# Splitting the router off the second norm in a transformer block: raw logit rows, a shift row through DRAM, and a gather by token tiles

## The chip, the cores and the metric

The kernel runs on one core of a Trainium2 chip. The metric is the device time in microseconds (us), the median of three runs. The engines are PE (TensorE), DVE (VectorE), ACT (ScalarE), POOL (GpSimd) and SP (SyncE, here only a queue of DMA issues).

## The reference, cut to what matters

One layer on 256 tokens of width 1024: an adaptive norm, a sparse attention branch and a gated linear attention branch, then a mixture of 32 experts, 4 for each token. Float32 throughout. The change lies at the seam between the branches and the experts:

```python
mod = (silu(c) @ w_ada + b_ada)                      # sh1, sc1, gt1, sh2, sc2, gt2, 1024 wide each
x = x + gt1 * (merged @ w_out)
h2 = _rmsnorm(x, norm2_g) * (1.0 + sc2) + sh2
x = x + gt2 * _moe(h2, ...)

def _moe(h, ...):
    logits = xt @ router_w + router_b
    top_v, top_e = lax.top_k(logits, TOP_K)          # TOP_K = 4 of 32
    wts = softmax(top_v)
    ... tokens sorted by expert; for each block of one expert:
        hgu = xb @ w_gate_up[e] + b_gate_up[e]       # 1024 -> 2048
        act = (min(gate, 7) * sigmoid(1.702 * gate)) * (clip(up) + 1)
        y = act @ w_down[e] + b_down[e]              # 1024 -> 1024
```

The expert weights are 12 MB for each expert, 384 MB in all, and every expert is read.

## The kernel before

The kernel is written engine by engine with semaphores set by hand. 256 tokens are two tiles of 128 (t = 0, 1), the width is two halves of 512. A list PLAN gives the order in which PE fills the eight PSUM banks by name (`wo0`, `hh0`, `rl1`, ...) and says whether ACT or DVE takes each out.

**Front part.** SP loads the weights in pieces of 2 MB into four buffers; each piece waits until PE (or DVE, for the `ada` pieces) has used the one before it in its buffer (L397). DVE multiplies the eight `ada` pieces of the six modulation rows by silu(c) (`weigh`, L1066), PE adds the partitions up with a matrix of ones (`add_parts`, L1549; tiles `ab0` to `ab7`) and DVE adds the bias (`take_sum`, L1021): `ab0`, `ab1` give gt1, `ab2`, `ab3` the shift sh2, `ab4`, `ab5` the scale sc2g, `ab6`, `ab7` the gate gt2.

**The seam.** PE makes `wo0` and `wo2` (token tile 0), then `wo1` and `wo3` (tile 1), L1574. `take_wo` (L1047) on DVE forms the residual x2 and x2 times sc2g. ACT takes the sum of squares (`square_sum`), `second_norm` (L1056) makes the inverse root and the finished rows h2. PE transposes h2 (`hh0` to `hh3`), multiplies with the router's weights in four row groups (`rp`), ACT copies the partial sums (`rpart`) and PE adds them up (`rl`, L1598). DVE picks the top four (`chosen`), PE counts (`rt`), DVE finds the slot of each token with expert 0 (`sel`, L1164), and PE gathers the rows of expert 0's block (`gather`, L1613). PE matmuls called `keep_busy` fill its waits. `router_weights` (L1147) makes the softmax weights; POOL splits them into three bf16 parts (L553 to L558) and only then begins to copy experts. h2 is also split in three bf16 parts, by `round_part` on ACT and `subtract_part` (L1114) on DVE.

**The experts.** Expert 0 comes in 12 loads of 1 MB straight into its slots. Each later expert comes in six units of 2 MB into three landing buffers in turn (`land`, L391), and POOL copies each unit in two halves into the slots (L566) as PE is done with them. The unit after next can only be issued when POOL has emptied its landing buffer. The first three units wait for other things: unit 0 for all of h2 and the gate, unit 1 for `rl1`, unit 2 for `gather` and for `left` of both tiles (L1120). Units 3, 4 and 5 wait for POOL's copies of units 0, 1 and 2. A loop over blocks of 64 rows then runs `gate_up` (L1688) and `down` (L1738).

Of the kernel before, what the change touches and what calls it, by code (L numbers as in the profile page):

```python
# [15 lines left out]
P = 128  # L16
# [54 lines left out]
def hybrid_block(nc, x, c, w_ada, b_ada, norm1_g, w_in, w_gate_lr, b_gate, gla_norm_g, w_branch_a, w_branch_b, w_out,  # L71
# [27 lines left out]

    with ExitStack() as ctx:  # L100
# [13 lines left out]
        bd = sb("bd", 96, [P, D])  # L114
# [45 lines left out]
        gt2 = sb("gt2", 180, [P, D])  # L160
# [56 lines left out]
        wts4 = sb("wts4", 187.5, [P, TT, 2, E])  # L217
# [6 lines left out]
        rpart = sb("rpart", 152, [P, T])  # L224
        first_used = small("first_used", [1, 1], I32)
# [55 lines left out]
        landing = [sb(f"landing{i}", at, [P, 2, 2048]) for i, at in enumerate((168, 152, 104))]  # L281
        fgl = sb("fgl", 168, [P, D])
# [34 lines left out]
        first_count_ready = sem("first_count_ready")  # L317
        gu_used = [sem(f"gu_used{j}") for j in range(8)]
# [56 lines left out]
        def _(sp):  # L375
# [94 lines left out]
        def _(pool):  # L470
# [31 lines left out]
            for part, dst in ((2, gt1), (3, sh2), (5, gt2), (4, fgb)):  # L502
                pool.dma_start(dst[:], b_ada[0:1, part * D:(part + 1) * D].to_broadcast([P, D])).then_inc(brow_in, 16)
# [4 lines left out]
            for i in range(4):  # L508
                pool.dma_start(bd[E * i:E * (i + 1), :], b_down[0]).then_inc(bd_in, 16)
# [33 lines left out]
            pool.wait_ge(bias3_ready, 1)  # L543
            for q in range(2):
                step.settle()
                step(nc.gpsimd.tensor_copy(gt2q[64 * q:64 * q + 64, :], gt2[64 * q:64 * q + 64, 512 * q:512 * q + 512]), gate_ready)
            pool.wait_ge(bd_in, 64)
            step.settle()
            step(nc.gpsimd.tensor_tensor(bd[:], bd[:], gt2[:], ALU.mult), gate_ready)

            pool.wait_ge(wts_ready, TT)
# [24 lines left out]
        def _(act):  # L576
# [256 lines left out]
        def _(dve):  # L833
# [184 lines left out]
            dve.wait_ge(brow_in, 64)  # L1018
            chain(V.scalar_tensor_tensor(fgb[:], fgb[:], 1.0, sc2g[:], ALU.add, ALU.mult))

            def take_sum(r):  # L1021

                cols_ = slice(512 * (r % 2), 512 * (r % 2) + 512)
                dst = (gt1, sh2, sc2g, gt2)[r // 2][:, cols_]
                wait_tile(dve, f"ab{r}")
                if r // 2 == 2:
                    chain(V.tensor_tensor(dst, tile(f"ab{r}")[:], dst, ALU.mult))
                    step(V.tensor_tensor(dst, dst, fgb[:, cols_], ALU.add), out_dve)
                else:
                    step(V.tensor_tensor(dst, tile(f"ab{r}")[:], dst, ALU.add), out_dve)  # L1030


# [14 lines left out]
            def take_wo(i):  # L1047
                cc, t = divmod(i, TT)
                xv = xs[:, t, 512 * cc:512 * cc + 512]
                wait_tile(dve, f"wo{i}")  # L1050
                chain(V.tensor_tensor(tmp[:], tile(f"wo{i}")[:], gt1[:, 512 * cc:512 * cc + 512], ALU.mult), out_dve)
                chain(V.tensor_tensor(x2[t][cc][:], xv, tmp[:], ALU.add), x2_ready)
                cols_ = slice(512 * cc, 512 * cc + 512)
                step(V.tensor_tensor(h2[:, t, cols_], x2[t][cc][:], sc2g[:, cols_], ALU.mult))

            def second_norm(t):  # L1056
# [3 lines left out]
                inverse_root(1, D, (x2ss_ready, 2 * t + 2), x2var_ready, x2root_ready, first=t)  # L1060
                for half in range(2):
                    cols_ = slice(512 * half, 512 * half + 512)
                    step(V.scalar_tensor_tensor(h2[:, t, cols_], h2[:, t, cols_], rs[:, t:t + 1], sh2[:, cols_],
                                                ALU.mult, ALU.add), h2_ready)
# [59 lines left out]
            subtract_part(1, 0)  # L1124
            take_wo(3)
            second_norm(1)
# [3 lines left out]
            for i in range(3):  # L1130
                step(V.memset(ypart[i][:], 0.0), ypart_ready[i])
            step(V.memset(zrow[:], 0.0), zrow_ready)
            dve.wait_ge(numbers_ready, 1)
            step(V.tensor_scalar(esel[:], ones[0:3 * E, 0:SLOTS], expert_no[:], None, ALU.is_gt), esel_ready)

            step(V.memset(lg[:, :, E:E + TOP_K], PAD))
# [10 lines left out]
            def router_weights(t):  # L1147
# [7 lines left out]
                step(V.tensor_copy(wts4[:, t, :, :], wts[:, t, :].unsqueeze(1).to_broadcast([P, 2, E])), wts_ready)  # L1155

            router_weights(0)
            wait_tile(dve, "rt")
            for t in range(TT):
                step(V.scalar_tensor_tensor(first_slot[:, t:t + 1], tile("rt")[:, t * E:t * E + 1], 1.0, chosen[:, t, 0, 0:1],  # L1160
                                            ALU.add, ALU.mult))
            step.settle()
            for t in range(TT):
                ins = V.tensor_scalar(sel[:, t, :], slot_no[:], first_slot[:, t:t + 1], None, ALU.is_equal)  # L1164
            ins.then_inc(sel_ready, 1)
# [21 lines left out]
            router_weights(1)  # L1187
# [3 lines left out]
            subtract_part(0, 1)  # L1191
# [7 lines left out]

            subtract_part(1, 1)  # L1200
# [23 lines left out]
            dve.wait_ge(gate_ready, 3)  # L1224
# [57 lines left out]
        def _(pe):  # L1282
# [61 lines left out]
            def transposes(name, src, t, half):  # L1344
                ps = begin(name)
                for j in range(4):
                    a = (4 * half + j) * P
                    ins = nc.tensor.transpose(ps[:, j * P:(j + 1) * P], src[:, t, a:a + P], ident[:])
# [199 lines left out]

            def add_parts(r):  # L1549
# [13 lines left out]
            for kind, src in (("gm", hT), ("wa", yaT), ("wb", ybT)):  # L1563
                for cc in range(2):
                    by_feature(kind, cc, src)
                    add_parts(r - 1)
                    r += 1
            pe.wait_ge(merged_ready, 4)
            for t in range(TT):
# [6 lines left out]
                if t == 0:  # L1576
                    add_parts(7)

            pe.wait_ge(late_in, 48)
            pe.wait_ge(bias3_ready, 1)  # L1580
            for t in range(TT):
                if t:
                    keep_busy(tile("rp0"), 4)
                for half in range(2):
                    pe.wait_ge(h2_ready, 2 * t + half + 1)
                    transposes(f"hh{2 * t + half}", h2, t, half)
                ps = begin(f"rp{t}")
                keep_busy(ps, 3 if t else 7)
# [7 lines left out]
                M(ps[:, 0:E], ones[0:1, :], rb[:], start=True, stop=False)  # L1596
                wait_out(pe, f"rp{t}")
                full(M(ps[:, 0:E], rpart[:, t * P:(t + 1) * P], stack[:], start=False, stop=True))  # L1598

            ps = begin("rt")  # L1600
            keep_busy(ps, 5)
            pe.wait_ge(chosen_ready, 1)
            M(ps[:, 0:E], before[:], chosen[:, 0, 0, :], start=True, stop=True)
            M(ps[:, E:3 * E], ones[:], chosen[:, 0, 0:2, :], start=True, stop=False)
            pe.wait_ge(chosen_ready, 2)
# [7 lines left out]
            def gather(into):  # L1613

                for t in range(TT):
                    for q in range(2):
                        ins = M(into[64 * q:64 * q + 64, :], sel[:, t, :], h2[:, t, 512 * q:512 * q + 512],
                                start=(t == 0), stop=(t == TT - 1))
                ins.then_inc(gath_full, 1)
# [31 lines left out]
            def weight_transposes():  # L1651

                pe.wait_ge(wts_ready, TT)
                nc.tensor.transpose(x_bank[:, 0:P], wts4[:].rearrange("p t q e -> p (t q e)"), ident[:]).then_inc(wt_full, 1)
# [16 lines left out]
            def bias_rows():  # L1671

                for i in range(4):
                    t, q = divmod(i, 2)
                    M(sum_bank[t][q][:], wT[E * i:E * (i + 1), :], bd[E * i:E * (i + 1), 512 * q:512 * q + 512], start=False, stop=False,
# [78 lines left out]
            pe.wait_ge(gate_ready, 3)  # L1754
# [35 lines left out]
```

## Time and profile before

| | us |
|---|---|
| median of 3 runs (lowest, highest) | 1346.03 (1345.78, 1346.28) |
| profiled execution | 1347.94 |
| its span, first to last instruction | 1346.2 |
| PE busy | 1320.4 (98%) |
| POOL busy | 703.6 (52%) |
| DVE busy | 478.4 (36%) |
| ACT busy | 300.9 (22%) |
| DMA's part of the chain that ended last | 56% of the span |
| granted TensorE clock | 0.995 of full |

The span is the time from the first to the last instruction of the profiled execution. The chain that ended last is followed back from the last instruction, at each step to what released it.

### The profile page before, as it was taken

Reading aid. Unit: us, or ns where it says so; the run is one execution under the profiler, and the core shown is the slowest. Engines: PE = TensorE matmul, PEld = TensorE weight load, DVE = VectorE, ACT = ScalarE, POOL = GpSimd, SP = SyncE. Lnnn points to the kernel's source line nnn. Section 1 sums busy time; section 2 is a strip of 40 time slices with the busy share of each in tenths; the row PEclk is TensorE's granted clock in tenths of the full one; section 3 lists DMA queues with packets and bytes.
Section 4 is the critical chain, followed back from the end, with each engine's and each line's share of the span. In section 5 each row is a group of like instructions: output and inputs, shape, how many; then the busy total and the mean of one; then the engine's idle time right before and its main releaser. Section 6 shows DMA issues by size and latency. Waiting matters only on the chain.

```text
span 1346.2 us, 18076 instructions
## 1 busy us (share of the span) xinstructions
PE 1320.4 (98%) x6683; PEld 620.1 (46%) x6684; DVE 478.4 (36%) x862; ACT 300.9 (22%) x577; POOL 703.6 (52%) x430
## 2 busy tenths in 40 slices
PE   7999999999999999999999999999999999999996
PEld 3888545788844333333333333333333333333332
DVE  1160006355578324223233242333332333233332
ACT  2320004310023222222122122222222222222222
POOL 1000000010015777767777687777777777777771
PEclk9999999999999999999999999999999999999998
DMA  9735333499959999999999999999999999999995
GB/s 339 279 127 186 125 125 125 161 322 367 329 219 382 429 428 429 428 403 429 428 428 428 428 409 429 428 428 428 407 431 428 428 428 407 430 428 428 428 427 231
DMA packets 70818, 483.79 MB, mean 359 GB/s; under 512 B 7270, under 2 KB 7466, under 8 KB 44970
## 3 DMA queue, kind: packets, MB, share of 16 engines
q1 hardware_dynamic: 69250, 478.20, 86.8%
q0 software_dynamic: 1056, 3.93, 1.0%
q10 hardware_dynamic: 488, 1.33, 0.3%
q8 instruction: 16, 0.26, 0.1%
q14 instruction: 8, 0.07, 0.0%
HBM read 482.40 MB, written 1.05 MB: 359 GB/s over the span
## 4 chain that ended last, share of the span: by engine, by line
DMA 56%; PE 34%; POOL 4%; issue 3%; DVE 1%; SPq 1%; ACT 1%; POOLq 0%; DVEq 0%; ACTq 0%
DMA landing<-in_w_gate_up 41%; PE bank L1332 15%; DMA landing<-in_w_down 14%; PE bank L1341 6%; POOL gu_slot L566 3%; PE bank L1688 3%; PE bank L1738 3%; PE bank L1574 2%; DMA piece<-in_w_ada 2%; SPq L397 1%; PE bank L1660 1%; PE bank L1553 0%; PE bank L1478 0%; PE bank L1705 0%; SPq L391 0%
## 5 line engine op out<-in xcount | busy, mean ns | idle before, releaser
L566 POOL COPY gu_slot<-landing 128x2048 f32<-128x2048 f32 x246 | 458.8, 1895 | 145.0 <-issue 107.9
L1688 PE MATMUL bank<-gu_slot,xg 128*64 128x512 f32 x2304 | 509.4, 593 | 3.2 <-POOL gu_slot L566 2.8
L1688 PEld LDWEIGHTS bank<-gu_slot,xg 128*64 128x64 f32 x2304 | 164.3, 137 | 320.5 <-issue 298.4
L566 POOL COPY dn_slot<-landing 128x2048 f32<-128x2048 f32 x120 | 223.5, 1894 | 71.2 <-issue 53.6
L1738 PE MATMUL bank<-dn_slot,actT 128*64 128x512 f32 x1152 | 255.1, 595 | 0.0
L1332 PE MATMUL bank<-hT,piece 128*128 128x256 f32 x704 | 153.4, 379 | 0.0
L1738 PEld LDWEIGHTS bank<-dn_slot,actT 128*64 128x64 f32 x1152 | 79.5, 137 | 159.2 <-issue 158.7
L1332 PEld LDWEIGHTS bank<-hT,piece 128*128 128x128 f32 x704 | 133.4, 190 | 19.1 <-issue 1.1
L812 ACT ACTIVATE ypart<-bank 128x512 bf16<-128x512 f32 x105 | 62.7, 597 | 313.8 <-DVE bank L1241 260.2
L1230 DVE TENSOR_SCALAR bank<-bank 128x512 f32<-128x512 f32 x36 | 25.2, 700 | 283.6 <-PE bank L1688 283.6
L1241 DVE SCALAR_TENSOR_TENSOR bank<-bank,slot_w,gt2q 128x512 f32<-128x512 f32 x35 | 26.6, 759 | 238.8 <-PE bank L1738 238.8
L796 ACT ACTIVATE sig<-bank 128x512 f32<-128x512 f32 x36 | 21.5, 597 | 321.3 <-PE bank L1688 321.3
L1341 PE MATMUL bank<-piece,hT 128*128 128x512 f32 x192 | 83.2, 593 | 0.0
L496 POOL TENSOR_SCALAR_AFFINE_SELECT AT<-AT 64x512 f32<-64x512 f32 x2 | 1.3, 660 | 124.8 <-ACT AT L591 124.7
L1258 DVE TENSOR_TENSOR bank<-bank,ypart 128x512 f32<-128x512 f32 x70 | 49.0, 699 | 46.4 <-ACT ypart L812 46.4
L500 POOL DMA_DIRECT2D sc2g<-in_norm_g x1 | 0.7, 723 | 121.1 <-PE bank L1504 121.1
L1660 PE MATMUL bank<-ypart,selT 64*128 64x512 bf16 x432 | 59.1, 379 | 0.0
L1341 PEld LDWEIGHTS bank<-piece,hT 128*128 128x128 f32 x192 | 36.3, 190 | 44.4 <-issue 44.3
L1205 DVE TENSOR_SCALAR pick<-slot_no,slot_id 128x64 bf16<-128x64 f32 x70 | 54.8, 826 | 5.3 <-DVE slot_no L1248 0.5
L1705 PE MATMUL bank<-part,pick 128*64 128x512 bf16 x420 | 51.3, 379 | 0.0
L796 ACT ACT_TABLE_LOAD x35 | 44.9, 1283 | 1.3 <-issue 0.7
L1075 DVE SCALAR_TENSOR_TENSOR modq<-piece,csig,modq 128x512 f32<-128x512 f32 x56 | 42.1, 752 | 2.0
(342 smaller groups left out, 986.8 us busy)
## 6 DMA issues: line engine op xcount, KB each, us to landing
landing<-in_w_gate_up SPq DMA_DIRECT2D x123, 2048.0 KB, 10.7
landing<-in_w_down SPq DMA_DIRECT2D x60, 2048.0 KB, 10.7
piece<-in_w_in SPq DMA_DIRECT2D x17, 2048.0 KB, 7.7
piece<-in_w_ada SPq DMA_DIRECT2D x12, 2048.0 KB, 13.2
gu_slot<-in_w_gate_up SPq DMA_DIRECT2D x10, 1024.0 KB, 7.1
dn_slot<-in_w_down SPq DMA_DIRECT2D x8, 1024.0 KB, 13.8
piece<-in_w_branch_a SPq DMA_DIRECT2D x2, 2048.0 KB, 9.3
piece<-in_w_branch_b SPq DMA_DIRECT2D x2, 2048.0 KB, 8.1
```

The source lines that it names most:

```text
L566: nc.gpsimd.tensor_copy(place, landing[j // 2 % 3][:, j % 2, :]).then_inc(there, 16)
L796: A(sig[:], gu_bank[0][:], ACT.Sigmoid, scale=ALPHA).then_inc(sig_ready, 1)
L812: A(ypart[i][:], a_bank[:], ACT.Copy).then_inc(ypart_ready[i], 1)
L1075: chain(V.scalar_tensor_tensor(dst[:], w[:, k, :], csig[:, k:k + 1], dst[:], ALU.mult, ALU.add), modq_ready if k == KT - 1 else None)
L1205: ins = V.tensor_scalar(pick[:, t, :], slot_no[:], slot_id[:, t, ds(e, 1)], None, ALU.is_equal)
L1258: V.tensor_tensor(a_bank[:], a_bank[:], ypart[i][:], ALU.subtract).then_inc(yrest_ready[i + 1], 1)
L1332: ins = M(ps[:, f * T:(f + 1) * T], w[:, k, a:a + P], src[:, k, :], start=(k == 0), stop=(k == KT - 1))
L1341: ins = M(ps[:], src[:, k, t * P:(t + 1) * P], w[:, k, :], start=(k == 0), stop=(k == KT - 1))
L1660: ins = M(sum_bank[t][q][:], selT[64 * q:64 * q + 64, t * P:(t + 1) * P], ypart[i][64 * q:64 * q + 64, :], start=False, stop=False)
L1688: ins = M(gu_bank[u][64 * q:64 * q + 64, :], xg[:, k % 4, 64 * (k // 4):64 * (k // 4) + 64], gu_slot[k][:, cols_], start=(k == 0), stop=(k ...
L1705: ins = M(x_bank[64 * q:64 * q + 64, :], pick[:, t, :], part[i][:, t, 512 * q:512 * q + 512], start=(t == 0 and i == 0), stop=(t == TT - 1 ...
L1738: ins = M(a_bank[64 * q:64 * q + 64, :], actT[:, f % 4, 64 * (f // 4):64 * (f // 4) + 64], dn_slot[f // 2][:, f % 2, 512 * q:512 * q + 512 ...
```

## The change

- **The router from rows without norm.** A logit is rs times (x2 * sc2g) @ router_w plus (sh2 @ router_w + router_b), where rs is the inverse root of the token. The transposes `hh0` to `hh3` now take x2 * sc2g (for tile 0 from a new buffer `u0`), and DVE applies rs and the constant row `cb` when it takes the logits. The PE order of the router's part becomes hh2, hh0, hh1, hh3, rp0, rl0, rp1, rl1, and most of its `keep_busy` matmuls are gone (14 before `rl1` become none, 5 and 3 behind it become 3, 2 and 2).
- **The constant row.** POOL stores row sh2 to DRAM and, when that has landed, loads it back as a column `shc` of 1024 single floats. PE forms `hc` (nine one-row matmuls) in the place of `ab6`, DVE copies it (`rb2`), PE spreads it over the partitions, DVE copies it again (`cb`).
- **The gather by tiles.** Each tile has its own rank matmul into a bank of its own and its own slot comparison (`first_slots`); the gather of tile 0 runs before that of tile 1. The finished h2 of tile 1 (`norm_rows(1)`) moves behind the top four and the slots of tile 0. Both `router_weights` move behind `br`, both tile 1 `subtract_part` move later.
- **The gate in halves.** `ab6` and `ab7` become one tile with half 0 on partitions 0 to 63 and half 1 on 64 to 127, taken out once; POOL's two copies to `gt2q` go, and its product with `b_down` is on 512 columns for 1024.
- Landing buffers 0 and 1 swap places; unit 0 now waits for `rl1`, unit 1 for all of h2. Two memsets of `ypart` move from DVE to POOL behind `wo3`.

```diff
-            sp.wait_ge(h2_ready, 4)
-            sp.wait_ge(gate_ready, 3)
-            land(E - 1, 0)
-            wait_tile(sp, "rl1")
+            wait_tile(sp, "rl1")
+            land(E - 1, 0)
+            sp.wait_ge(h2_ready, 4)
+            sp.wait_ge(gate_ready, 1)
             land(E - 1, 1)
...
+            wait_out(pool, "ab3")
+            pool.dma_start(shift_store[:], sh2[0:1, :]).then_inc(shift_out, 16)
+            pool.wait_ge(shift_out, 16)
+            pool.dma_start(shc[:], shift_store[0].rearrange("(k p) -> p k", p=P), allow_slow_non_contiguous=True).then_inc(shc_in, 16)
...
+            take_T(h2T, "hh", 2)
+            square_sum(1, 1)
             take_T(h2T, "hh", 0)
+            norm_root(1)
             take_T(h2T, "hh", 1)
-            square_sum(1, 1)
-            norm_root(1)
+            take_T(h2T, "hh", 3)
             take_partial(0)
-            take_T(h2T, "hh", 2)
-            take_T(h2T, "hh", 3)
             take_partial(1)
...
+            wait_tile(dve, "hc")
+            step(V.tensor_copy(rb2[:], tile("hc")[0:1, 0:E]), out_dve)
             weigh(7)
-            take_sum(6)
             take_wo(0)
             take_wo(2)
-            take_sum(7)
-            second_norm(0)
+            take_gate()
+            dve.wait_ge(row_full, 1)
+            step(V.tensor_copy(cb[:], tile("hc")[:, 64:64 + E]), row_out)
+            step.settle()
+            norm_scale(0)
+            norm_rows(0)
...
-                chain(V.tensor_copy(lg[:, t, 0:E], tile(f"rl{t}")[:, 0:E]), out_dve)
+                chain(V.scalar_tensor_tensor(lg[:, t, 0:E], tile(f"rl{t}")[:, 0:E], rs[:, t:t + 1], cb[:], ALU.mult, ALU.add), out_dve)
...
-            router_weights(0)
+            def first_slots(t, ranks_):
+
+                chain(V.scalar_tensor_tensor(first_slot[:, t:t + 1], ranks_, 1.0, chosen[:, t, 0, 0:1], ALU.add, ALU.mult))
+                V.tensor_scalar(sel[:, t, :], slot_no[:], first_slot[:, t:t + 1], None, ALU.is_equal).then_inc(
+                    sel_ready if t else sel0_ready, 1)
+
+            dve.wait_ge(rank0_full, 1)
+            first_slots(0, bank[6][:, 0:1])
+            norm_rows(1)
+            dve.wait_ge(rank1_full, 1)
+            first_slots(1, bank[5][:, 0:1])
...
-            router_weights(1)
             wait_tile(dve, "br")
...
-            subtract_part(0, 1)
+            router_weights(0)
+            router_weights(1)
...
-            subtract_part(1, 1)
+            subtract_part(0, 1)
...
             chain(V.tensor_copy(table[:], tile("te")[0:1, 0:ends[5]]), tables_ready)
+            subtract_part(1, 1)
...
+            def add_gate_parts():
+
+                ps = begin("ab7")
+                pe.wait_ge(modq_ready, 8)
+                for q in range(2):
+                    ins = M(ps[64 * q:64 * q + 64, :], ones[:, 0:64], modq[q][:], start=True, stop=True)
+                full(ins)
...
+            pe.wait_ge(late_in, 48)
+            pe.wait_ge(shc_in, 16)
+            ps = begin("hc")
+            for k in range(KT):
+                M(ps[0:1, 0:E], shc[:, k:k + 1], wr[:, k, :], start=(k == 0), stop=False)
+            full(M(ps[0:1, 0:E], ones[0:1, 0:1], rb[:], start=False, stop=True))
...
-            wait_out(pe, "rl0")
-            keep_busy(bank[6], 3)
+            wait_out(pe, "rl1")
+            pe.wait_ge(sel0_ready, 1)
+            gather(x_bank, 0)
+            keep_busy(bank[7], 2)
             pe.wait_ge(sel_ready, 1)
-            gather(x_bank)
+            pe.wait_ge(h2_ready, 4)
+            gather(x_bank, 1).then_inc(gath_full, 1)
```

## Rows read from the trace of the kernel before

**Rows 1.** Busy us of PE, PEld, DVE, ACT, POOL by stretch; PEclk, DMA share, GB/s

```profile
400.00:402.00 2.00, 2.00 (x16) 0.97 (x18) 1.73 (x3) 1.81 (x4) 0.00 (x0) 1.00 0.69 168
402.00:416.00 14.00, 13.34 (x101) 7.38 (x102) 12.18 (x76) 6.00 (x12) 1.16 (x2) 1.00 1.00 407
416.00:426.00 10.00, 10.00 (x59) 3.69 (x56) 9.66 (x15) 2.62 (x3) 9.46 (x8) 1.00 0.91 320
426.00:434.00 8.00, 8.00 (x52) 3.30 (x49) 6.49 (x8) 1.19 (x2) 6.73 (x5) 1.00 0.98 397
440.00:1312.00 872.00, 870.09 (x4664) 320.34 (x4660) 286.78 (x445) 202.00 (x377) 660.72 (x355) 1.00 1.00 425
```

**Rows 2.** SP's queue in time: units 0 and 1, 2, 3; expert 2's units 1 and 2

```profile
405.12 3.07 SPq L391 DMA_DIRECT2D landing<-in_w_gate_up  x2
...
416.19 0.33 SPq L391 DMA_DIRECT2D landing<-in_w_gate_up  x1
...
422.45 0.33 SPq L391 DMA_DIRECT2D landing<-in_w_gate_up  x1
...
441.15 4.22 SPq L391 DMA_DIRECT2D landing<-in_w_gate_up  x2
```

**Rows 3.** The chain that ended last, 400 to 421 us: start, duration, what

```profile
400.09 1.09 ACT h2T L591 x2
...
401.27 0.73 ACT junk L743 x2
...
407.42 0.42 PE bank L1598 x2
...
407.87 0.20 DVE lg L1139
...
408.83 0.27 DVE chosen L1144
...
410.38 0.42 DVE sel L1164 x2
...
413.46 0.24 DVE ranks L1186
...
414.50 0.21 DVE wts L1155
...
418.50 1.94 POOL gu_slot L566
```

**Rows 4.** DVE and POOL in order of time: second norm, splits, casts, slots

```profile
403.68 1.41 DVE L1063 SCALAR_TENSOR_TENSOR h<-h,rs,sh 128x512 f32<-128x512 f32 x2
...
414.89 1.23 DVE L1120 TENSOR_TENSOR left<-h,part 128x1024 f32<-128x1024 f32 x1
...
415.24 1.07 POOL L556 TENSOR_TENSOR wrest<-wts,wpart 128x64 f32<-128x64 f32 x1
...
416.86 0.33 POOL L556 TENSOR_TENSOR wrest<-wrest,wpart 128x64 f32<-128x64 f32 x1
...
417.24 1.23 DVE L1118 TENSOR_TENSOR part<-left,part 128x1024 bf16<-128x1024 f32 x1
...
419.11 1.37 DVE L1221 SCALAR_TENSOR_TENSOR slot_id<-slot_id,chosen 128x32 f32<-128x32 f32 x1
...
428.44 1.84 DVE L1205 TENSOR_SCALAR pick<-slot_no,slot_id 128x64 bf16<-128x64 f32 x2 [0.16 <-DVE slot_no L1248]
```

**Rows 5.** DVE and PE in order of time: sh2 finished, `ab6`, the first `wo` matmuls

```profile
332.10 0.69 DVE L1030 TENSOR_TENSOR sh<-bank,sh 128x512 f32<-128x512 f32 x1
...
369.28 1.02 PE L1553 MATMUL bank<-modq,ones 128*128 128x512 f32 x2
371.02 1.55 PE L1574 MATMUL bank<-piece,mergedT 128*128 128x512 f32 x3 [0.72 <-DVE mergedT L1044]
```

**Rows 6.** DMA issues: the load of `wsm` in 1024 rows of 128 B, us to landing

```profile
wsm<-in_w_in SPq DMA_DIRECT2D x1, 128.0 KB, 12.1
```

**Rows 7.** Landing time of unit 2 (issued at 416.19 us), from the landing buffers' view

```profile
DMA to landing us min/median/max: 7.6/7.6/7.6
```

More of the change, by code:

```diff
@@ L224, in hybrid_block @@
         rpart = sb("rpart", 152, [P, T])
+        u0 = sb("u0", 128, [P, D])
+        shc = small("shc", [P, KT])
+        rb2 = small("rb2", [1, E])
+        cb = small("cb", [P, E])
         first_used = small("first_used", [1, 1], I32)
@@ L500, in _ @@
             pool.dma_start(sc2g[:], norm2_g[0:1, :].to_broadcast([P, D])).then_inc(g2_in, 16)
[L502 removed]
+            for q in range(2):
+                a = 5 * D + 512 * q
+                pool.dma_start(gt2b[64 * q:64 * q + 64, :], b_ada[0:1, a:a + 512].to_broadcast([64, 512])).then_inc(brow_in, 16)
+            for part, dst in ((2, gt1), (3, sh2), (4, fgb)):
                 pool.dma_start(dst[:], b_ada[0:1, part * D:(part + 1) * D].to_broadcast([P, D])).then_inc(brow_in, 16)
@@ L542, in _ @@
             wait_out(pool, "ab7")
[L543 to L546, printed above, removed]
             pool.wait_ge(bd_in, 64)
             step.settle()
-            step(nc.gpsimd.tensor_tensor(bd[:], bd[:], gt2[:], ALU.mult), gate_ready)
+            step(nc.gpsimd.tensor_tensor(bd[:], bd[:], gt2q[:], ALU.mult), gate_ready)
+            wait_tile(pool, "wo3")
+            for i in range(2):
+                step(nc.gpsimd.memset(ypart[i][:], 0.0), ypart_ready[i])
             pool.wait_ge(wts_ready, TT)
@@ L1030, in take_sum, with take_gate @@
                     step(V.tensor_tensor(dst, tile(f"ab{r}")[:], dst, ALU.add), out_dve)
+            def take_gate():
+                wait_tile(dve, "ab7")
+                step(V.tensor_tensor(gt2q[:], tile("ab7")[:], gt2b[:], ALU.add), out_dve)
             def take_wa(i):
@@ L1060, in second_norm, with norm_rows @@
                 inverse_root(1, D, (x2ss_ready, 2 * t + 2), x2var_ready, x2root_ready, first=t)
+            def norm_rows(t):
                 for half in range(2):
                     cols_ = slice(512 * half, 512 * half + 512)
-                    step(V.scalar_tensor_tensor(h2[:, t, cols_], h2[:, t, cols_], rs[:, t:t + 1], sh2[:, cols_],
-                                                ALU.mult, ALU.add), h2_ready)
+                    step(V.scalar_tensor_tensor(h2[:, t, cols_], h2[:, t, cols_] if t else u0[:, cols_], rs[:, t:t + 1],
+                                                sh2[:, cols_], ALU.mult, ALU.add), h2_ready)
             def weigh(r):
@@ L1129, in _ @@
             step(V.memset(selT[:], 0.0), selw_out)
-            for i in range(3):
-                step(V.memset(ypart[i][:], 0.0), ypart_ready[i])
+            step(V.memset(ypart[2][:], 0.0), ypart_ready[2])
             step(V.memset(zrow[:], 0.0), zrow_ready)
+            subtract_part(1, 0)
             dve.wait_ge(numbers_ready, 1)
             step(V.tensor_scalar(esel[:], ones[0:3 * E, 0:SLOTS], expert_no[:], None, ALU.is_gt), esel_ready)
+            take_wo(3)
+            norm_scale(1)
             step(V.memset(lg[:, :, E:E + TOP_K], PAD))
@@ L1154, in router_weights @@
                 chain(V.tensor_scalar(wts[:, t, :], wts[:, t, :], rt_b[:, t:t + 1], None, ALU.mult))
-                step(V.tensor_copy(wts4[:, t, :, :], wts[:, t, :].unsqueeze(1).to_broadcast([P, 2, E])), wts_ready)
-            router_weights(0)
-            wait_tile(dve, "rt")
[L1159 to L1165, printed above, removed]
+                step(V.tensor_copy(wts4[:, :, t, :], wts[:, t, :].unsqueeze(1).to_broadcast([P, 2, E])), wts_ready)
+            def first_slots(t, ranks_):
[7 more added lines that the diff above has]
+            first_slots(1, bank[5][:, 0:1])
+            wait_tile(dve, "rt")
             counts, counts_col = tile("rt")[:, TT * E:TT * E + E], tile("rt")[0:3 * E, (TT + 1) * E:(TT + 1) * E + 1]
@@ L1576, in _ @@
                 if t == 0:
-                    add_parts(7)
+                    add_gate_parts()
+                    wait_out(pe, "hc")
+                    M(tile("hc")[:, 64:64 + E], ones[0:1, :], rb2[:], start=True, stop=True).then_inc(row_full, 1)
             pe.wait_ge(late_in, 48)
             pe.wait_ge(bias3_ready, 1)
-            for t in range(TT):
[L1582 to L1586, printed above, removed]
+            pe.wait_ge(u_ready, 3)
+            transposes("hh2", h2, 1, 0)
+            pe.wait_ge(row_out, 1)
+            transposes("hh0", u0, None, 0)
+            transposes("hh1", u0, None, 1)
+            pe.wait_ge(u_ready, 4)
+            transposes("hh3", h2, 1, 1)
+            for t in range(TT):
                 ps = begin(f"rp{t}")
-                keep_busy(ps, 3 if t else 7)
                 for r in range(2):
@@ L1611, in _, with gather @@
             full(ins)
[L1613 to L1619, printed above, removed]
+            def gather(into, t):
+                for q in range(2):
+                    ins = M(into[64 * q:64 * q + 64, :], sel[:, t, :], h2[:, t, 512 * q:512 * q + 512],
+                            start=(t == 0), stop=(t == TT - 1))
+                return ins
             def gather_transposes(into):
```

54 lines of the change are left out of this document (30 added, 24 removed), and 4 rows, old and new, of the table PLAN.

## The prediction

> **What bounds the kernel now.** The page comes first: its chain that ended last is more DMA than anything else. The busy times by stretch say where: from 440 to 1312 us the DMA engines are full at 425 GB/s [rows 1], so the kernel ends when the expert weights have come in, plus a tail of 34 us from 1312 to 1346.2 that the change leaves alone. Everything ahead of 440 us matters only by how early the stream is full. The same view shows where it is not: against the 425 GB/s, the bytes missing are worth 1.2 us of stream in 400 to 402, 0.6 us in 402 to 416, 2.5 us in 416 to 426 and 0.5 us in 426 to 434 [rows 1] (for example (425 - 320) / 425 x 10 us). That is 4.8 us, and it is the most that any reordering of the seam can win, as long as PE's `wo` matmuls end no earlier, which nothing here makes them do.
>
> SP's queue in time says why the holes are there [rows 2]. Unit 2 is issued at 416.19 us, when unit 1 is nearly in, and unit 3 at 422.45 us. Unit 2 had the stream to itself and landed after 7.6 us [rows 7]; 2.1 MB at 425 GB/s are 4.9 us of that, so 2.7 us pass with no bytes of it. The last hole is therefore set by unit 3, and it by POOL's first two copies of 1.94 us, the first at 418.50 us. The chain of waits goes back from there [rows 3]: DVE's softmax weights end at 414.71, the ranks at 413.70, `sel` at 410.80, the top four at 409.10, `rl1` at 407.84, the last square sum at 402.00. The reader is to see that two chains leave the router, one through `sel` to the gather and PE, the other through the weights to POOL, and that the stream hangs on POOL's.
>
> **The change, part by part.** All times are places in the profiled execution.
>
> Constant row. `ab6` falls away (its passes reach 0.86 us beyond wb3's, shown as 1.02), and nine one-column matmuls stand there; PE waits there for the merge anyway until 371.02 [rows 5]. No pass of the same shape is in my rows; nine matmuls of two passes at no more than half of 0.42 us each (L1598) [rows 3] bound it at 3.8 us, nothing at the lower end; I take under 1.5 us, hidden by that wait, since 32 columns are a sixteenth of `ab6`'s 512. Above that it would be on PE's path one for one, to +2.3 us. DVE's two small copies of `rb2` and `cb` (0.2 us each, as `lg` [rows 3]) lie where DVE waits for `wo` tiles. The store and the load through DRAM can start at 332.8 us, when sh2 is whole, and must be in by about 370 [rows 5]: 37 us. The store is put at unit 2's 7.6 us [rows 7], the load at the 12.1 us of 1024 rows of 128 B beside a full stream [rows 6]; with issue about 22 us. POOL does nothing else meanwhile. Cost 0, cover 15 us.
>
> The gate in halves. `ab7` is two half-width matmuls of 512 columns for one of full width at 1.02 us [rows 5]. Side by side they cost nothing, one after the other 0.9 us; a one-row matmul follows, 0 to 0.42 us [rows 3]. I take +0.3 us for the end of `wo3`, near the low end because the gate_up matmuls already run in such pairs. POOL's shorter work ends long before it is needed: 0.
>
> Router. The last square sum takes 0.73 us after x2 [rows 3]; it began at 401.27 because ACT was copying, and may now begin at 401.1 + 0.3 = 401.4 and end at 402.15. ACT then does three copies of 0.54 us (half of 1.09), the root and two partial sums of about 0.3 us; PE's `rl0` and `rl1` take 0.42 us each, partly beside them. `rl1` ends at about 402.15 + 1.62 + 0.2 + 0.6 + 0.84 + 0.6 of hand-overs = 406.0, 1.8 us earlier than 407.84. The top four take 1.23 us as before (407.87 to 409.10 [rows 3]) and end at 407.3.
>
> Slots. Before, `sel` came 1.70 us behind the top four. Now DVE does the slots of tile 0 (0.45 us, two short operations), both halves of `norm_rows(1)` (1.41 us [rows 4]) and the slots of tile 1 (0.45 us): `sel` at 409.65, 1.15 us earlier than 410.80. PE's gather and gate_up of expert 0 follow, 1.1 to 1.4 us earlier. That shift has no receiver: PE is no releaser of unit 3.
>
> Weights. From `sel` to the ranks is 2.90 us [rows 3], so 412.55. Behind it DVE now has first_col (0.35 us) and both `router_weights` at 1.0 us (413.70 to 414.71 for one): 414.9, against 414.71. The 1.15 us won are spent on the weights of tile 0 that used to lie in a wait: +0.2 us for POOL.
>
> Splits. `subtract_part(0, 1)`, 1.23 us, moves behind of_block. `left` of tile 1 and with it unit 2 come at 414.9 + 1.1 + 1.23 = 417.2 for 416.19: +1.0 us. Units 0 and 1 come at 406.1 and 409.2 for 405.12 and 407.9. Their two gaps grow, but the stream's place is reset at unit 3, which already starts with nothing ahead of it, so I charge them nothing. Queued behind the later `left` are SP's units 3 to 5, all later anyway.
>
> POOL and DVE on one port. Before, the weights' end and the first copy are 3.79 us apart [rows 3]. In them both splits meet POOL's casts: `wrest` takes 1.07 us beside the first and 0.33 us alone, and the first copy begins where the second split ends (417.24 + 1.23 = 418.47) [rows 4]. Later the copies hold DVE: `slot_id` takes 1.37 us until copy 0 ends [rows 4]. Now the first split still meets the casts (416.0 to 417.2), the second does not, which gives back about 0.45 us: first copy at 414.9 + 3.34 = 418.25. But `subtract_part(1, 1)` now stands behind the table, is ready at about 418.3 and gets its turn between copy 0 and copy 1: 1.23 us on POOL. Unit 3: 418.25 + 1.94 + 1.23 + 1.94 and the 0.07 us of issue seen before = 423.43, against 422.45: +1.0 us. Bounds: no split meets POOL's work, and the stream can gain only until unit 2's own end (417.2 + 7.6 = 424.8, then 4.9 us for unit 3 = 429.7, against 422.45 + 7.6 = 430.05), -0.4 us; the casts stay as slow as before (+0.45) and `wo3` ends 1.3 and not 0.3 us late (both gate halves in a row and the row matmul, +1.0), +2.4 us. I take +1.0, since both splits stand where these rows put them.
>
> Here a rule of the Trainium skill stands against the easy reading that short DVE work beside POOL is free (SBUF - State Buffer, "SBUF: two separate sides"): VectorE and GpSimd share a port pair by an exclusive lock held for the whole instruction, the loser blocks. The two durations of `wrest` agree; without the rule the sum would be the +0.2 us of the weights, with it +1.0 us. The page adds that a two-input VectorE operation is locked only against a GpSimd operation that reads SBUF; by that the two memsets moved to POOL beside `take_wo(3)` cost nothing.
>
> Late next: the second split and the six blocked DVE operations behind it put `pick` (428.44 to 430.28 [rows 4]) at about 431.5. PE's first `down` is then 0.6 us later, and its slots free landing buffers for the units issued from 441.15 [rows 2]. They queue behind two others, so some 2.9 us of lateness are covered.
>
> Other edits (landing buffers swapped, `bias_rows` in another order, smaller loads before 300 us where PE sets the pace): 0.
>
> **Sum.** +0.2 (weights) - 0.45 (second split off the casts) + 1.23 (on the copies) = +1.0 us. The profiled execution took 1347.94 us, its span is 1346.2; it would become 1348.9. The median of the runs is 1.9 us below that execution, so 1346.03 + 1.0 = 1347.0 us. Differences under 0.2% (2.7 us) are about what a measurement of this kernel can't tell from none.
>
> **Rivals.**
> - The early router reaches the stream. If the weights or the copies in fact follow `rl1` (1.8 us earlier) and the splits fall into gaps, units 3 to 5 follow and the holes of 4.8 us close in part: 1341.5 to 1344.5. For: every step up to the top four is shorter. Against: both `router_weights` now lie in a row. Chance 0.12, nearly all of it beyond 0.2%.
> - Slower by the column. `hc` waits for `shc`; if it lands after 370 us every microsecond goes one for one through `wo3` to the end. It decides from 15 us of lateness against my 22 us. At 378 us it is +8, 1354. For: 1024 single floats on POOL's queue, and no row of such a load. The Trainium skill (same page and section) warns that descriptors of GpSimd's queue can't be written while VectorE holds the port. DVE's chain of `weigh` is dense there, but it has waits of 6 us between. Chance 0.07.
> - The port costs more: further DVE operations between POOL's copies, `pick` late by over 2.9 us, so that unit 1 of expert 2 starts late. +2 to +5 us, 1349.5. Chance 0.07.
> - The clock. It is 1.00 throughout the seam [rows 1]; 14 of the filler matmuls are gone. At 1.2 GHz the gather and the first part of gate_up would double; gate_up paces POOL's copies at nearly their own speed, +2 to +4 us. PE is never idle much over 1 us there. Chance 0.03.
>
> **The numbers.** The forecast, with its own range 1345.6 to 1348.4, has 0.71. Faster by over 0.2%: 0.11 from the first rival. Slower: 0.07 + 0.05 + 0.02 and the far end of my own bounds, 0.15. Within: 0.74. The range 1343.6 to 1349.4 takes in both bounds of the port and the near part of the first rival, and leaves out the column.
>
> **What would show it.** `rl1` near 406.0; `sel` near 409.7; weights near 414.9; unit 2 at 417.2; unit 3 at 423.4; DMA still 425 GB/s from about 440; `hc` without a wait. Wrong if unit 3 is issued before 421.5 or after 425.5, if PE waits for `shc`, or if holes appear in the stream behind 440 us.

## The result: slower by 0.29%, and the profile after

Over 20 executions each, the changed kernel takes 1352.18 us in the median (1346.38 to 1355.07) and the kernel before 1346.47 us (1344.79 to 1350.28). The ratio is 1.0029, 95% interval 1.0018 to 1.0041. The forecast was 1347.0 us, no change.

The 20 times are not one cluster. Eleven lie from 1351.94 to 1355.07 us and show a mean granted TensorE clock of 0.988 to 0.992; nine lie from 1346.38 to 1349.86 us at 0.994 to 0.997. The profiled execution (1346.38 us, span 1344.7) is of the nine, so its trace shows the change at a full clock. The busy times by stretch, columns as in [rows 1]:

```profile
400.00:402.00 2.00, 1.45 (x20) 0.75 (x20) 1.43 (x8) 1.95 (x6) 0.00 (x0) 1.00 0.94 369
402.00:416.00 14.00, 12.76 (x92) 6.91 (x94) 10.95 (x58) 5.15 (x10) 2.28 (x4) 1.00 0.96 385
416.00:426.00 10.00, 10.00 (x49) 3.24 (x47) 9.27 (x9) 2.19 (x3) 9.38 (x7) 1.00 0.94 330
426.00:434.00 8.00, 6.72 (x50) 2.95 (x48) 6.77 (x11) 2.51 (x7) 6.63 (x4) 1.00 1.01 430
...
440.00:1312.00 872.00, 870.18 (x4664) 320.42 (x4662) 286.89 (x445) 202.12 (x377) 660.72 (x355) 1.00 1.00 425
```

The stream is as full from 440 us as in [rows 1], and the holes are of the same kind. What looks different is PE's busy time: 1.45 of 2 us, 12.76 of 14 us and 6.72 of 8 us, for 2.00, 13.34 and 8.00 in [rows 1]. The clock column still reads 1.00.

SP's queue in time, the answer to [rows 2]: units 2 and 3.

```profile
415.61 0.33 SPq L399 DMA_DIRECT2D landing<-in_w_gate_up  x1
421.57 0.33 SPq L399 DMA_DIRECT2D landing<-in_w_gate_up  x1
```

And the chain that ended last, the answer to [rows 3]: DVE's first operation on `wo3`, the last square, `rl1`, the top four, the weights of tile 1, POOL's first copies.

```profile
398.18 0.70 DVE tmp L1071
...
399.63 0.72 ACT junk L758 x2
...
403.87 0.39 PE bank L1644 x2
...
405.31 0.26 DVE chosen L1170
...
413.24 0.20 DVE wts L1181
...
417.23 0.43 POOL gu_slot L581
...
419.65 1.90 POOL gu_slot L581
...
421.57 7.33 DMA landing<-in_w_gate_up
```

DVE takes `wo3` at 398.18 us, where the forecast had 399.95 (the front part came 1.5 us sooner in this execution, and moves by more than that from one to the next). Counted from there (399.65 us in the trace of before), the steps were:

| from DVE's take of `wo3`, us | before | forecast | after |
|---|---|---|---|
| `rl1` ends | 8.2 | 6.05 | 6.1 |
| top four of tile 1 | 9.4 | 7.35 | 7.4 |
| `sel` of tile 1 | 11.15 | 9.7 | 9.4 |
| weights of tile 1 | 15.1 | 14.95 | 15.3 |
| unit 2 issued | 16.5 | 17.25 | 17.4 |
| unit 3 issued | 22.8 | 23.5 | 23.4 |

At a full clock each step lies within 0.35 us of the forecast. The 5.7 us between the medians are not in this trace.

### The profile page after: what moved, and what is told of

Read it like the earlier page. It is cut to its first block, busy times and chain, and to the rows that moved or that the text cites. A ratio compares the mean times of both kernels' runs of the same rounds, so it can differ in the third digit from the quotient of the medians.

```text
span 1344.7 us, 18098 instructions
## 1 busy us (share of the span) xinstructions
PE 1317.6 (98%) x6690; PEld 618.9 (46%) x6691; DVE 476.2 (35%) x861; ACT 300.9 (22%) x577; POOL 705.4 (52%) x433
## 4 chain that ended last, share of the span: by engine, by line
PE 72%; DMA 23%; POOL 2%; issue 1%; DVE 1%; ACT 1%; SPq 0%; ACTq 0%; POOLq 0%; DVEq 0%
PE bank L1740 23%; DMA landing<-in_w_gate_up 17%; PE bank L1361 15%; PE bank L1790 12%; PE bank L1370 6%; DMA landing<-in_w_down 6%; PE bank L1712 3%; PE bank L1757 2%; PE bank L1618 2%; POOL gu_slot L581 1%; PE bank L1779 1%; PE bank L1339 1%; PE bank L1673 1%; PE bank L1747 1%; PE bank L1349 1%
## 5 line engine op out<-in xcount | busy, mean ns | idle before, releaser
L1740 PE MATMUL bank<-gu_slot,xg 128*64 128x512 f32 x2304 | 509.2, 593 | 3.1 <-POOL gu_slot L581 3.0
L1740 PEld LDWEIGHTS bank<-gu_slot,xg 128*64 128x64 f32 x2304 | 164.3, 137 | 320.2 <-issue 298.4
L1233 DVE TENSOR_SCALAR pick<-slot_no,slot_id 128x64 bf16<-128x64 f32 x70 | 48.4, 734 | 5.2 <-DVE slot_no L1277 0.8
```

Source lines behind the costliest of these rows:

```text
L1233: ins = V.tensor_scalar(pick[:, t, :], slot_no[:], slot_id[:, t, ds(e, 1)], None, ALU.is_equal)
L1740: ins = M(gu_bank[u][64 * q:64 * q + 64, :], xg[:, k % 4, 64 * (k // 4):64 * (k // 4) + 64], gu_slot[k][:, cols_], start=(k == 0), stop=(k ...
```

## The experiments

Each kernel was measured over 11 or 12 executions, beside 15 to 35 of the kernel before. The ratio compares these two sets and is not the quotient of the medians, so the two can differ a little.

### The changed kernel again

No edit. 

> The changed kernel unchanged. Its 20 times lie in two groups, 8 from 1346.4 to 1349.2 at a mean granted TensorE clock of 0.994 to 0.997 and 12 from 1349.9 to 1355.1, mostly at 0.988 to 0.992, and the profiled one is of the first. Theory C (TensorE's clock falls in some executions, and the seam then runs long): again both groups, and if the profile falls into the second, one stretch of 10 to 25 us between 366 and 450 shows a clock near 0.5 and the experts' stream is full 5 to 8 us later. Theory P (port order alone): no group by clock, times within 1 us of each other at 1347.

Measured: 1351.21 us in the median (1346.44 to 1355.32), ratio 1.0028 (1.0013 to 1.0043). Seven of 12 at 0.988 to 0.992 and 1351.0 us or more, five at 0.995 to 0.996 and 1348.6 us or less. This time the profiled execution is one of the long ones (1351.68 us, clock 0.991). Its busy times by stretch:

```profile
396.00:402.00 6.00, 5.08 (x28) 2.95 (x30) 4.31 (x9) 2.65 (x7) 0.98 (x2) 1.00 0.80 285
402.00:408.00 6.00, 4.78 (x55) 3.23 (x54) 4.59 (x24) 3.33 (x8) 0.00 (x0) 0.97 0.92 343
408.00:412.00 4.00, 4.00 (x14) 1.51 (x15) 3.19 (x20) 1.06 (x1) 0.00 (x0) 0.50 1.02 438
412.00:416.00 4.00, 4.00 (x12) 1.36 (x9) 0.25 (x2) 0.60 (x1) 0.00 (x0) 0.50 0.99 426
416.00:420.00 4.00, 4.00 (x13) 1.54 (x13) 3.50 (x16) 0.60 (x1) 1.75 (x3) 0.50 0.17 74
420.00:424.00 4.00, 4.00 (x27) 1.45 (x24) 1.27 (x3) 1.06 (x1) 3.02 (x4) 0.83 0.70 213
```

The clock column is to be read down: 0.97, then 0.50 (1.2 GHz for 2.4) from 408 to 420 us and back within the last row. In finer stretches it falls at about 407.7 and is back at about 421.4 us, some 14 us in all. Ahead of the fall PE was busy 5.08 and 4.78 us of two times 6, and much of that in short matmuls. The price stands in the last column: 74 GB/s from 416 to 420 us, a hole worth 3.3 of 4 us. PE in order of time shows the waits, and then the same matmuls at half speed:

```profile
401.31 0.66 PE L1377 MATMUL bank<-ident,h 128*128 128x128 f32 x4 [0.92 <-DVE h L1074]
...
403.35 0.38 PE L1644 MATMUL bank<-stack,rpart 128*128 128x32 f32 x2 [0.49 <-ACT rpart L606]
...
404.79 0.38 PE L1644 MATMUL bank<-stack,rpart 128*128 128x32 f32 x2 [0.49 <-ACT rpart L606]
...
408.81 1.97 PE L1666 MATMUL bank<-h,sel 128*64 128x512 f32 x4
...
417.95 3.60 PE L1740 MATMUL bank<-gu_slot,xg 128*64 128x512 f32 x8
```

In the full-clock trace the gather of tile 0 (L1666) took 1.08 and the first piece of gate_up 1.94 us. From DVE's take of `wo3` (399.11 us) to unit 3 (426.69 us) are 27.6 us here and 23.4 there, +4.2 us. What released POOL's two copies in this trace:

```profile
421.82 1.89 POOL L581 COPY gu_slot<-landing 128x2048 f32<-128x2048 f32 x1 [0.55 <-PE bank L1740]
424.76 1.90 POOL L581 COPY gu_slot<-landing 128x2048 f32<-128x2048 f32 x1 [1.05 <-PE bank L1740]
```

L1740 is `gate_up`: the second copy had to wait until PE had used its slot a second time. In the full-clock trace PE was done with it 2.1 us before the copy (417.5 and 419.65 us).

### The fillers put back into the router

```diff
+            wait_out(pe, "wo0")
+            keep_busy(tile("hh3"), 4)
             pe.wait_ge(u_ready, 4)
             transposes("hh3", h2, 1, 1)
...
                 ps = begin(f"rl{t}")
+                keep_busy(ps, 2)
                 wait_out(pe, f"rp{t}")
```

> The changed kernel with 8 filler matmuls put back into PE's waits of the router: 4 ahead of hh3, 2 ahead of each rl (idle of 0.93, 0.49 and 0.49 us there). Theory C with the router's gaps as its cause: the second group goes, all times 1346 to 1348, clock 0.994 or more. Theory C with another cause (the 1.3 us wait for pick ahead of the expert loop): both groups stay, half or more of the times over 1350. Theory P: nothing changes but up to 0.5 us later.

Measured: 1347.26 us (1345.19 to 1349.44), ratio 1.0001 (0.9992 to 1.0009), every execution at 0.994 to 0.998. The slowdown is gone, within the interval, with eight matmuls that compute nothing. The two stretches around the top four in its trace:

```profile
402.00:408.00 6.00, 5.76 (x61) 3.79 (x59) 4.71 (x25) 3.27 (x9) 0.00 (x0) 1.00 0.94 345
408.00:412.00 4.00, 4.00 (x20) 1.49 (x21) 2.95 (x20) 1.43 (x2) 0.00 (x0) 1.00 1.02 438
```

### Fillers at the other wait only

```diff
             pe.wait_ge(gate_ready, 1)
+            keep_busy(x_bank, 6)
             with pe.Fori(0, pe.snap(nb - 1)) as g:
```

> The changed kernel with 6 filler matmuls (1.3 us) ahead of the expert loop, where PE waits 1.28 us for pick. Theory C with this wait as its cause: all times 1346 to 1348, clock 0.994 or more. Theory C with the router's gaps as cause: both groups stay. Theory P: nothing changes.

Measured: 1354.6 us (1346.39 to 1356.24) in the median of 11 executions, ratio 1.0041 (1.0025 to 1.0057); a twelfth of 5586.65 us is left out. Seven of the 11 are at 0.988 to 0.991, from 1352.4 to 1356.2 us. The wait for `pick` is not the cause.

### The kernel before without its fillers ahead of `rl1`

```diff
-                if t:
-                    keep_busy(tile("rp0"), 4)
...
-                keep_busy(ps, 3 if t else 7)
```

> The kernel before without its 14 filler matmuls ahead of rl1; all else stays. Theory C with the router's gaps as cause: a second group of 1351 to 1356 at a clock of 0.988 to 0.992 appears, the median goes up by 4 to 7 us. Theory C with the wait for pick as cause, and theory P: as the kernel before, 1345 to 1348, median within 1 us.

Measured: 1351.15 us (1346.86 to 1356.43), ratio 1.0034 (1.0022 to 1.0046), 11 of 12 at 0.989 to 0.993. Nothing of the change but the loss of the fillers is in this kernel, and it has the change's slowdown. Its busy times by stretch:

```profile
396.00:402.00 6.00, 3.57 (x32) 2.22 (x31) 4.34 (x12) 2.17 (x6) 0.00 (x0) 0.99 0.77 287
402.00:408.00 6.00, 5.90 (x35) 3.40 (x33) 4.41 (x38) 4.26 (x8) 0.00 (x0) 0.50 1.02 381
408.00:412.00 4.00, 4.00 (x18) 2.65 (x18) 1.79 (x11) 0.06 (x1) 0.00 (x0) 0.50 1.00 426
```

PE was busy only 3.57 of 6 us, and the clock fell about 5 us behind DVE's take of `wo3` (396.82 us), for 8.6 us in the trace of the changed kernel. It was low for some 14 us here too. Unit 3 came 28.2 us behind that take, for 22.8 in the kernel before, and again PE's `gate_up` (L1685) released both copies:

```profile
420.02 2.05 POOL L566 COPY gu_slot<-landing 128x2048 f32<-128x2048 f32 x1 [2.97 <-PE bank L1685]
423.07 1.89 POOL L566 COPY gu_slot<-landing 128x2048 f32<-128x2048 f32 x1 [0.99 <-PE bank L1685]
```

### Which waits

Four more kernels leave out or put back the fillers in part.

```diff
 a_fill_hh3: only this in the changed kernel
+            wait_out(pe, "wo0")
+            keep_busy(tile("hh3"), 4)
 a_fill_rl: only this in the changed kernel
+                keep_busy(ps, 2)
 b_no_fill_7: the kernel before
-                keep_busy(ps, 3 if t else 7)
+                keep_busy(ps, 3 if t else 0)
 b_no_fill_4_3: the kernel before
-                if t:
-                    keep_busy(tile("rp0"), 4)
...
-                keep_busy(ps, 3 if t else 7)
+                keep_busy(ps, 0 if t else 7)
```

> The changed kernel with only the 4 fillers ahead of hh3 (the 0.93 us wait for the last quarter of x2 * sc2g). Theory C1 (the clock falls because of the router's idle time as a sum): some executions still at 0.988 to 0.992, fewer than in the changed kernel, median between 1347 and 1351. Theory C2 (this longest gap alone is the cause): no low clock, median 1347. Theory C3 (only the two waits ahead of rl matter): as the changed kernel, median 1351.

> The changed kernel with only the 2 fillers ahead of each rl (two waits of 0.49 us). C1: median between 1347 and 1351. C2: as the changed kernel, median 1351. C3: no low clock, median 1347.

> The kernel before without the 7 fillers of token tile 0 alone; the 4 and the 3 of tile 1 stay. C1: a part of the executions at 0.988 to 0.992, median between 1347 and 1351. Theory that only gaps near the top four count: as the kernel before, 1347.

> The kernel before without the 4 and 3 fillers of token tile 1; the 7 of tile 0 stay. Theory C1 (idle time of the router as a sum): some executions at 0.988 to 0.992, median 1347.5 to 1351. If the waits close ahead of the top four decide, more of them than without the 7 (none there).

| | fillers left ahead of `rl1` | median, us | ratio (interval) | executions at a mean clock of 0.993 or less |
|---|---|---|---|---|
| changed | none | 1351.21 | 1.0028 (1.0013 to 1.0043) | 7 of 12 |
| a_fill_hh3 | 4 ahead of hh3 | 1348.32 | 1.0022 (1.0008 to 1.0037) | 5 of 12 |
| a_fill_rl | 2 and 2 ahead of rl | 1347.73 | 1.0006 (0.9997 to 1.0015) | 1 of 11 |
| a_fill_router | 4, 2 and 2 | 1347.26 | 1.0001 (0.9992 to 1.0009) | 0 of 11 |
| b_no_fill | none | 1351.15 | 1.0034 (1.0022 to 1.0046) | 11 of 12 |
| b_no_fill_4_3 | 7 of tile 0 | 1350.58 | 1.0021 (1.0009 to 1.0034) | 8 of 12 |
| b_no_fill_7 | 4 and 3 of tile 1 | 1347.34 | 1.0003 (0.9994 to 1.0012) | 0 of 11 |

The longest gap (0.92 us ahead of hh3) is not the cause alone: filled, it leaves 5 of 12. The two short ones of 0.49 us, the last ahead of the top four, seem to weigh more (1 of 11 against 5 of 12, small counts), and in the kernel before the 4 and 3 of tile 1 weigh more than the 7 of tile 0 (8 of 12 against 0 of 11).

The last column misses short falls, though. The traces of a_fill_rl (1350.37 us) and of b_no_fill_7 (1347.9 us, mean clock 0.996, not counted in the column) both show 0.50 for some 3 us: from about 409.0 us, in the `gather`, and from about 402.6 us, ahead of `rl1`. Unit 3 came 1.5 and 1.4 us later behind the take of `wo3` than in the full-clock traces of the two kernels. In b_no_fill_4_3 the clock was low for some 10 us and unit 3 came 4.0 us later. So the 7 fillers of tile 0 may bear on the clock too: in the trace without them it fell, but was back before the `gather`. In these traces the cost grows with how far the low clock reaches into the `gather` and `gate_up`. Why it lasts 3 us in one trace and 14 in another, and how the chip decides, is not shown.

### Can the stream be made fuller at a held clock?

Three attempts at a version that beats both kernels. The first two turn POOL's order in the kernel with all 8 fillers and move `subtract_part(0, 1)` ahead of DVE's wait for `br`; the third does POOL's part in the kernel before. The cut of the edit leaves out the fillers.

```diff
+            pool.wait_ge(first_count_ready, 1)
+            first_free = pool.value_load(first_used[0:1, 0:1], min_val=1, max_val=MAXB + 1)
+            for j in range(2):              # range(1) in a_fill_copy_first
+                pool.wait_ge(unit_landed[0], 16)
+                pool.wait_ge(gu_used[j], first_free)
+                nc.gpsimd.tensor_copy(gu_slot[j][:], landing[0][:, j, :]).then_inc(gu_in[j], 16)
             pool.wait_ge(wts_ready, TT)
...
-            pool.wait_ge(first_count_ready, 1)
-            copy_units(1, pool.value_load(first_used[0:1, 0:1], min_val=1, max_val=MAXB + 1), 12)
+            copy_units(1, first_free, 12, 2)    # 12, 1 in a_fill_copy_first
...
+            subtract_part(0, 1)             # not in b_two_copies
             wait_tile(dve, "br")
...
-            subtract_part(0, 1)             # not in b_two_copies
```

> The changed kernel with all 8 fillers, and with POOL's order turned: the first copy of expert 1 ahead of the casts of the weights, and subtract_part(0, 1) ahead of DVE's wait for br. If units 3 to 5 hang on POOL's first copies, unit 3 is issued 1 to 2 us earlier from the end of wo3 than in the kernel with fillers alone, the hole in the stream between 416 and 426 us shrinks by as much, and the median goes from 1347.3 to 1345.3 to 1346.3. If PE's use of the slots holds the second copy, or DVE held by the first copy makes everything behind it late, the median stays within 0.5 us of 1347.3.

Measured: 1347.66 us (1346.61 to 1349.9), ratio 1.0008 (0.9999 to 1.0017). Unit 2 came early, at 411.65 us, but unit 3 only at 421.49 us, 23.2 us behind the take of `wo3`: the casts now stood between the two copies.

> As a_fill_copy_first, with both copies of unit 0 ahead of POOL's casts, since there the casts stood between copy 0 and copy 1. If unit 3 hangs on copy 1 and that on PE's second use of a slot (about 418 us), unit 3 is issued near 419.7 for 421.5, and the median is 1 to 2 us under a_fill_copy_first and a_fill_router (1347.3 to 1347.7), so 1345.5 to 1346.5, at or a little under the kernel before. If the casts, now later, hold units 4 and 5 or pick by as much, the median stays.

Measured: 1350.1 us (1346.53 to 1350.87), ratio 1.0019 (1.0011 to 1.0028). Unit 3 did come at 419.71 us, as expected, and the hole was smaller. But `pick` came late, and a hole opened again some 20 us later. PE in order of time, then the stretches behind it:

```profile
431.12 1.49 PE L1765 MATMUL bank<-part,pick 128*64 128x512 bf16 x12 [2.82 <-DVE pick L1238]
```

```profile
416.00:426.00 10.00, 10.00 (x49) 3.24 (x47) 7.68 (x9) 1.56 (x2) 8.48 (x10) 1.00 0.96 376
426.00:434.00 8.00, 5.18 (x38) 2.08 (x35) 6.92 (x9) 1.20 (x2) 6.75 (x4) 1.00 0.99 401
434.00:440.00 6.00, 6.00 (x34) 2.32 (x34) 0.47 (x3) 1.62 (x5) 2.54 (x2) 1.00 1.01 426
440.00:450.00 10.00, 10.00 (x50) 3.40 (x48) 4.33 (x6) 3.08 (x4) 8.54 (x5) 1.00 0.96 379
```

376 GB/s for the changed kernel's 330 in the first row, and then 379 from 440 to 450 where the rest of the stream has 425. This is one of the two fastest of the 12 executions (1347.06 us). Nine of them took 1349.1 us or more, at clocks of 0.994 to 0.996, and no trace shows what held those.

> The kernel before with both copies of unit 0 ahead of POOL's casts. By the same chain unit 3 comes up to 1 us earlier, no more, since PE's second use of a slot comes at about 420.4 there, and DVE's table chain is held by the copies: median within 1 us of the kernel before.

Measured: 1349.68 us (1348.17 to 1351.73), ratio 1.0025 (1.0016 to 1.0034): 3.1 us over the kernel before, where at most 1 us was expected. In its trace (1348.33 us, again one of the two fastest) PE stood idle for `pick` (5.20 us busy of 8 from 426 to 434) and the stream had 376 GB/s from 440 to 450.

The last kernel asks whether the wait for `pick` costs by the clock once the router's fillers are in. In a_fill_router the profiled execution (1348.87 us) waited 2.93 us for it, and the clock fell there too. It does not always: the same wait was 2.82 us in a_fill_two_copies and 2.99 us in a_fill_hh3, and both traces keep 1.00.

```profile
431.73 2.77 PE L1760 MATMUL bank<-part,pick 128*64 128x512 bf16 x12 [2.93 <-DVE pick L1233]
```

```profile
430.00:432.00 2.00, 0.27 (x2) 0.18 (x4) 2.00 (x2) 0.00 (x0) 1.63 (x1) 0.77 0.97 418
432.00:434.00 2.00, 2.00 (x12) 0.72 (x8) 1.56 (x3) 0.00 (x0) 1.47 (x1) 0.50 1.03 442
...
440.00:450.00 10.00, 10.00 (x52) 3.42 (x50) 3.67 (x5) 3.07 (x4) 10.00 (x6) 1.00 0.91 345
```

```diff
             pe.wait_ge(gate_ready, 1)
+            keep_busy(x_bank, 8)
             with pe.Fori(0, pe.snap(nb - 1)) as g:
```

> The changed kernel with the 8 fillers of the router and 8 more (1.7 us) ahead of the expert loop. In the kernel with the router's fillers alone the clock held in the router and PE then waited for pick, 0.994 to 0.998 over the whole. If that second wait costs time by the clock, the median falls by 0.5 to 1 us, to 1346.3 to 1346.8, the kernel before or just under it. If it costs nothing, the median stays at 1347.3 with no execution over 1350; then the change has no gain of its own at a held clock. Against it speaks nothing over 1350 in either case.

Measured: 1347.59 us (1346.59 to 1349.11), ratio 1.0004 (0.9995 to 1.0013). Nothing over 1350, and no gain over the router's fillers alone. No version here beats the kernel before.

## Why the prediction was wrong

**The step that failed** is the rival of the clock: "It is 1.00 throughout the seam ... 14 of the filler matmuls are gone ... PE is never idle much over 1 us there. Chance 0.03." Both halves misled. The 1.00 of [rows 1] was read off a kernel that had the fillers in, so it said nothing of the clock without them. And the idle time was weighed by its longest piece. The pieces were 0.92, 0.49 and 0.49 us, none over 1 us, as said, with small matmuls between. With them 18 of 32 executions of the changed kernel have a mean clock of 0.988 to 0.992; the one of these that was traced has 0.50 for some 14 us. The sum put the missing fillers at nothing. That they are the cause is shown from both sides: eight fillers in the changed kernel give 1.0001, and the kernel before without its 14 gives 1.0034.

**Its mechanism** was right, and its size too small. The rival said +2 to +4 us, by `gate_up` pacing POOL's copies. The traces at half clock show just that: PE's `gate_up` released the second copy in the changed kernel and both copies in the kernel before without fillers, and unit 3 came 4.2 and 5.4 us later. The times at a mean clock of 0.991 to 0.992 lie 4 to 5 us over the full-clock ones, those at 0.988 to 0.989 some 7 us. No trace shows one of the latter; if 0.991 stands for 14 us at 0.50, then 0.988 stands for some 21 us (an estimate from the mean clocks).

There is a second path, which the prediction did not have. Both `router_weights` now stand behind DVE's wait for `br`, which PE makes behind the `gather`. DVE waits 0.65 us there at a full clock and 3.83 us in the trace at half clock, where the weights of tile 1 come 18.9 us behind the take of `wo3` and not 15.3. But moving them back would not have brought unit 3 forward in that trace, since PE's second use of the slot ended only at 424.6 us. The kernel before without fillers has no such wait ahead of its weights (18.0 us behind the take), and lost as much. No experiment separates the two paths.

The other steps, in the prediction's order:

- **What bounds the kernel**: right. The stream has 425 GB/s from 450 us on in every trace, and the holes lie ahead of it. Those between 440 and 450 us in a_fill_router and the two-copies kernels are what the prediction called a sign of being wrong.
- **Constant row**: right, with more cover than said. The store landed in 6.1 and the load in 3.9 us (7.6 and 12.1 were taken). From the list of DMA issues:

```profile
shift_store<-sh POOLq DMA_DIRECT2D x1, 4.0 KB, 6.1
shc<-shift_store POOLq DMA_DIRECT2D x1, 4.0 KB, 3.9
```

  The load landed at about 341.2 us, 26 us before PE used it (367.22); the rival of the late column never came near. `hc` took 0.8 us, hidden by PE's wait for the merge.
- **Gate in halves**: +0.3 us were taken. The two half matmuls and the row matmul hold PE for 1.01 and 0.33 us, where `ab7` held it for 0.86: +0.5 us.
- **Router, slots, weights**: right within 0.35 us in each line of the table above. In the weights two errors nearly cancel: the ranks came 0.3 us sooner than forecast, and DVE's 0.65 us for `br` was in no term. "PE is no releaser of unit 3" holds at a full clock, where the router that ends 2 us earlier gains nothing (1.0001). It was closer than the prediction saw: in the trace of before PE finished its second use of the slot at 420.3 us and the copy began at 420.5. At half clock it is false, and this is how the low clock reaches the stream.
- **Port**: the sum was near by luck, its terms were not. The casts did end 3.2 us behind the weights, sooner than before, though the first split still lengthened one from 0.4 to 1.4 us. But POOL then spent 0.55 us on reading the count ahead of the first copy, which before had run beneath the last cast, so that copy stayed 3.8 us behind the weights (forecast 3.3). The second split ran beside the start of copy 0, which took 2.47 us for 1.94, and so cost 0.5 us and not 1.23. Counted from `wo3`, unit 3 came 0.6 us later than before; the table's forecast was 0.7.
- **Late next**: `pick` was put 1.2 us later. Counted from `wo3` it came 0.7 us later in the full-clock trace, where PE waits 1.28 us for it without harm. In a_fill_hh3 it came 2.4 us later, at a full clock, and the stream has 402 GB/s from 440 to 450 us. In a_fill_router it came 2.2 us later, the clock fell too, and the stream has 345 GB/s, a loss worth 1.9 us. So the cover was less than the 2.9 us taken, and the rival "the port costs more" is real in that execution, which took 1.6 us more than its median.
- **The medians**: the other groups of the changed kernel, 1346.4 to 1349.9 us, have a median of 1347.1 and are what the forecast of 1347.0 describes. The median of all is of the long group, and with chances this close to even the side it falls on is partly luck.

The prediction also forecast one number for a kernel that has two groups of times. Where the mean clock of the executions differs by 0.008, a median over three can fall on either side.

## What to carry to other kernels

Filler matmuls are part of a schedule, not leftovers. When a change shortens or reorders a stretch that holds them, count PE's idle time again, short gaps too, ask which transfer waits for PE if its matmuls take twice as long, and look at the mean clock of all executions, not only at the profiled one. A clock of 1.00 in the profile of the kernel with fillers is no evidence for the kernel without.

A shorter path pays only if the transfer that sets the pace hangs on it. Here the router became 2 us shorter and the stream hung on POOL's first two copies. Pulling those forward, as a_fill_two_copies did, moved a hole in its trace to the next wait, `pick`, and the median went up.

## What the hardware showed that was not expected

- Idle pieces of 0.92 and twice 0.49 us on PE, between small matmuls, came ahead of a granted clock of 0.50 for some 14 us in the traced execution, and of a mean clock of 0.992 or less in about every second execution of one and the same program. Four fillers of 0.2 us each in the two short gaps brought that to 1 in 11. Shorter falls of some 3 us, in two other traces, hardly show in the mean clock (0.996 in one).
- A column of 1024 single floats, loaded from DRAM on GpSimd's queue, landed in 3.9 us, with 237 GB/s in all moving from 337 to 342 us.
- The same wait for `pick` was 1.28 us in one trace and 2.93 us in another that differs only in eight fillers ahead of it; the second half of `pick` on VectorE took 0.25 us in the one and 1.91 us, the length of a GpSimd copy, in the other. The Trainium skill (SBUF - State Buffer, "SBUF: two separate sides") has the port pair that VectorE and GpSimd share locked for a whole instruction. The traces agree: `slot_id`, with two inputs, takes 1.66 us beside a copy, and 0.19 us without one in the trace of the kernel before without fillers.
